# The prompt's group norm in two halves, the first under the last attention units, and output rows that begin two loop steps earlier

## The chip, the core and the metric

The kernel runs on one core of a Trainium2 chip. The metric is the device time in microseconds of one execution. A core has the engines TensorE (PE; PEld is its weight load), VectorE (DVE), ScalarE (ACT), GpSimd (POOL) and SyncE (SP), and 16 DMA engines that all of the queues share. An "x2" or "x16" of matrix rows counts instructions; one float32 matmul of the source shows as two.

## What is computed

One layer of a decoder over a prompt of 256 tokens and 8 sample tokens with a paged cache of 2048 tokens each. Heads 0 to 7 are stick-breaking ("sb"), heads 8 to 15 forgetting attention ("fox"). The part that matters here:

```python
def merge_heads(o_sb, o_fx, g_sb, g_fx, w_out):
    B, S = o_sb.shape[:2]
    o = jnp.concatenate([rms_norm(o_sb.reshape(B, S, D_SB), g_sb),
                         rms_norm(o_fx.reshape(B, S, D_FOX), g_fx)], axis=-1)
    return jnp.einsum('bse,ed->bsd', o, w_out)
...
    hp = hp + yp
    hs = hs + ys
    u = jnp.concatenate([rms_norm(hp, norm_ffn_g[l]).reshape(B * S, D),
                         rms_norm(hs, norm_ffn_g[l]).reshape(DB * DS, D)], axis=0)
    f = hier_moe(u, w_rg, b_rg, w_re, b_re, w_gate, w_up, w_down)
```

Each half of the concatenated heads has a norm of its own over its 1024 values per token. After the projection come the residual, a second norm, the routing (one of 4 groups, two of its 8 experts) and 32 experts, in float32.

## The kernel before

The middle of the kernel is one loop of 128 steps (STEPS), written out in Python for every engine, one step for each page of the sample tokens' cache: 8 sequences of 16 pages. An engine executes its own list in order and meets the others only at semaphores, so "step s" is a place in each engine's list and not a time.

In each step s:

- SP loads value page s (from s = 4, L109 to L116) and then key page s + 20 (L99 to L106), 0.5 MB for each head group, so 2 MB in a step. Both rings in SBUF hold four pages. The load of value page p waits until TensorE has used page p - 4, that of key page p until VectorE has scored page p - 4.
- TensorE multiplies value page s by the sample weights (`values`, L964).
- VectorE scores key page s + 20 against the broadcast queries (`score_page`, L128, sixteen instructions), before all else of its step. At the start of a sequence it waits for new queries (the copies by ACT at L146 of the broadcast by TensorE at L136, in step 11 of each sequence; for page 96 that is step 75).

Around these pages the prompt is worked off. Steps 0 to 71 project heads. From step UNIT0 = 16 to 79 there are 16 units of four steps (`prompt_head`): one head of causal attention, two sb heads, then two fox heads, in turn. Units 12 and 13 are the last sb heads (their outputs are copied to `qo` by step 71), 14 and 15 (steps 72 to 75 and 76 to 79) the last fox heads. A unit's last piece adds to semaphore `oc`. ACT also issues the stores of the unit's key and value rows (L1273, L1274), in pieces 1 and 2.

Then, before the change:

- step 80 (GSUM - 1): ACT squares both halves of `qo` into `xn` (L1320, waiting for all 16 units);
- steps 81 and 82: TensorE sums the squares of a half over heads and partitions, by a matrix of ones, into banks 2 and 3 (L1060);
- step 83 (GSUM + 2): VectorE takes the means (L1696), ACT the roots of both at once (L1385), VectorE the reciprocal (L1519) and 16 products in place in `qo` (L1521), one for each head;
- from step OUT = 84: `out_rows(o)` for o = 0 to 15, in two of every three steps (`out_at`), 32 matmul instructions each (L1084). o = 0 and 1 read heads 0 to 7 only, 2 and 3 heads 8 to 15, and so on in turn. Every second row step, ACT issues the next 2 MB of `w_out` (L177). VectorE adds the residual (L1527), ACT squares it (L1324), TensorE sums (L1065);
- from OUT_END = 107 the sums end, from ROUTE = 111 routing, from PLACE = 122 the placing of tokens. In steps 108 to 127 SP has only value pages left to load.

After the loop: the last sample output, the tokens of the first experts, the sample tokens' own projection, and then a second block of code with the experts, which streams 192 MB of weights. BANK R is 4 of TensorE's result banks; it holds unit rows until semaphore `row` shows that they are copied.

## Time and profile before

| | |
|---|---|
| Time, median of 3 runs | 1517.79 us (1516.69 to 1523.81) |
| Span of the profiled execution | 1514.3 us |
| TensorE, VectorE, ScalarE busy | 87%, 44%, 15% of the span |
| DMA | 377 GB/s on average, 570.4 MB in all |
| Squares (step 80) to the last output row (step 106) | 709.6 to 893.0 us |
| Last value page used | 947 us |

The span is that of one execution under the profiler; its own time is not listed beside it, and the runs are 2.4 us and more above it. The page cuts the span into 40 slices with the busy share of each engine in tenths, the granted clock of TensorE, and the share and rate of the DMA engines; the trace gives the same for any stretch. A share of the DMA engines can pass 1.00 a little, since packets overlap; 1.03 is the most that a long stretch shows.

### The profile page before, as it was taken

To read this page: it belongs to the slowest core of one execution; us is meant where nothing else is said; L and a number is where in the kernel's file an instruction comes from. 1 tells how busy PE (TensorE), PEld (TensorE's weight loads), DVE (VectorE), ACT (ScalarE), POOL (GpSimd) and SP (SyncE) were. 2 spreads that over 40 slices of the span, in tenths; PEclk is the share of its full clock that TensorE was granted. 3 is DMA by queue.
4 is the path that set the end of the run, shared out by engine and by line. 5 is a ranking of instruction groups with operands and counts; after the bars stand their busy time and mean duration, and the time that the engine had idled before them with its cause. 6 is when DMAs were issued, how large, how long until landed. Compare 5 with 4: busy or idle time off the path is not lost. (4 is left out here: it accounts for less than half of the span.)

```text
span 1514.3 us, 26133 instructions
## 1 busy us (share of the span) xinstructions
PE 1315.7 (87%) x8622; PEld 870.3 (57%) x8622; DVE 673.4 (44%) x4778; ACT 233.6 (15%) x453; POOL 75.4 (5%) x119
## 2 busy tenths in 40 slices
PE   7999788889789899856899987789999999999992
PEld 4678455566556566533667743466666565655561
DVE  4437855676676675677846466021000100000004
ACT  2111002112212212213011021101111010111011
POOL 1000000000000000001000001001100010001000
PEclk8899989899999999976999998979999999999997
DMA  9776999999999999999999989999999999999984
GB/s 302 248 260 229 385 397 391 396 383 381 382 377 390 383 379 392 387 405 398 351 403 402 401 320 390 399 414 379 422 428 428 427 424 423 422 419 414 416 341 178
DMA packets 170382, 570.39 MB, mean 377 GB/s; under 512 B 17401, under 2 KB 75562, under 8 KB 156954
## 3 DMA queue, kind: packets, MB, share of 16 engines
q1 hardware_dynamic: 145616, 541.70, 91.4%
q10 hardware_dynamic: 21762, 22.58, 4.3%
q0 software_dynamic: 2896, 4.86, 0.9%
q8 instruction: 45, 0.74, 0.2%
q14 instruction: 63, 0.52, 0.1%
HBM read 558.26 MB, written 15.67 MB: 379 GB/s over the span
## 5 line engine op out<-in xcount | busy, mean ns | idle before, releaser
L128 DVE CUSTOM_DVE_ANT_0 ws<-ws,xgT 128x128 f32<-128x128 f32 x1792 | 387.8, 284 | 204.7 <-DMA ws<-in_cache_fox_k 186.0
L979 PE MATMUL bank<-xn,ws 128*128 128x264 f32 x1152 | 289.9, 407 | 10.5 <-DMA ws<-in_w_in 10.5
L979 PEld LDWEIGHTS bank<-xn,ws 128*128 128x128 f32 x1152 | 223.0, 199 | 110.9 <-issue 54.8
L1912 PE MATMUL bank<-ws,xgT 128*64 128x256 f32 x1024 | 231.4, 386 | 16.7 <-DMA ws<-in_w_expert_up 12.1
L1914 PE MATMUL bank<-ws,xgT 128*64 128x256 f32 x1024 | 231.5, 386 | 0.0
L964 PE MATMUL bank<-ws,PR 128*32 128x512 f32 x1024 | 150.8, 668 | 78.3 <-DMA ws<-in_cache_fox_v 73.8
L1912 PEld LDWEIGHTS bank<-ws,xgT 128*64 128x64 f32 x1024 | 140.3, 139 | 104.6 <-issue 22.2
L128 DVE DVE_READ_ACCUMULATOR2_ANT Z<- 128x1 f32 x1792 | 141.8, 79 | 0.0
L1914 PEld LDWEIGHTS bank<-ws,xgT 128*64 128x64 f32 x1024 | 140.3, 139 | 0.0
L2113 DVE COPY gu<-bank 128x256 f32<-128x256 f32 x32 | 13.6, 425 | 269.4 <-PE bank L1914 269.4
L1084 PE MATMUL bank<-qo,ws 128*128 128x256 f32 x512 | 117.0, 387 | 6.2 <-DVE qo L1521 5.2
L1934 PE MATMUL bank<-ws,hT 128*32 128x512 f32 x1024 | 113.2, 594 | 7.1 <-ACT xgT L2012 6.9
L1084 PEld LDWEIGHTS bank<-qo,ws 128*128 128x128 f32 x512 | 97.7, 193 | 31.5 <-issue 16.6
L1901 PE MATMUL bank<-xg,qo 128*128 128x128 f32 x960 | 109.7, 275 | 0.0
L1901 PEld LDWEIGHTS bank<-xg,qo 128*128 128x128 f32 x960 | 108.5, 192 | 0.0
L964 PEld LDWEIGHTS bank<-ws,PR 128*32 128x32 f32 x1024 | 21.5, 112 | 119.8 <-DMA ws<-in_cache_fox_v 91.8
L523 PE MATMUL bank<-xn,ws 128*128 128x264 f32 x384 | 86.8, 387 | 0.0
L523 PEld LDWEIGHTS bank<-xn,ws 128*128 128x128 f32 x384 | 72.6, 190 | 14.1 <-issue 2.0
L1934 PEld LDWEIGHTS bank<-ws,hT 128*32 128x32 f32 x1024 | 32.0, 110 | 76.7 <-issue 67.0
L607 DVE CUSTOM_DVE_ANT_0 ws<-ws,xgT 128x128 f32<-128x128 f32 x256 | 55.3, 287 | 39.5 <-DMA ws<-in_cache_sb_k 15.6
L2120 DVE TENSOR_TENSOR hT<-si,bank 128x128 f32<-128x128 f32 x32 | 9.2, 288 | 108.3 <-ACT si L2020 108.2
L1848 POOL DMA_INDIRECT y_rows<-ys,dest x32 | 29.5, 922 | 403.6 <-DVE ys L2124 338.6
(433 smaller groups left out, 971.4 us busy)
## 6 DMA issues: line engine op xcount, KB each, us to landing
ws<-in_cache_sb_k SPq DMA_DIRECT2D x128, 512.0 KB, 9.1
ws<-in_cache_fox_k SPq DMA_DIRECT2D x128, 512.0 KB, 13.0
ws<-in_cache_sb_v SPq DMA_DIRECT2D x128, 512.0 KB, 9.2
ws<-in_cache_fox_v SPq DMA_DIRECT2D x128, 512.0 KB, 12.8
ws<-in_w_expert_gate SPq DMA_DIRECT2D x32, 2048.0 KB, 16.1
ws<-in_w_expert_up SPq DMA_DIRECT2D x32, 2048.0 KB, 20.0
ws<-in_w_expert_down SPq DMA_DIRECT2D x32, 2048.0 KB, 16.9
ws<-in_w_in SPq DMA_DIRECT2D x24, 2048.0 KB, 21.3
```

The lines of the kernel that those rows point to most:

```text
L128: ins = dve.tensor_tensor_reduce(k, k, qb[:, (g * H + h) * HD:(g * H + h + 1) * HD], 1.0, 0.0, ALU.mult, ALU.add, Z[:, n % 2, g, h, t:t + 1])
L523: mm = pe.matmul(bank[4 + k % 4][:, 0:T], chunk(n)[:, c, m * P:(m + 1) * P], xn[:, c, :], start=(c == 0), stop=(c == KC - 1))
L607: ins = dve.tensor_tensor_reduce(k, k, qb[:, (g * H + h) * HD:(g * H + h + 1) * HD], 1.0, 0.0, ALU.mult, ALU.add, Z[:, 0, g, h, t:t + 1])
L964: mm = pe.matmul(bank[0][r0:r0 + 32, :], PR[:, g, t, :], vring[:, u, g, half * 512:(half + 1) * 512], start=(t == 0), stop=(t == PAGES - 1))
L979: mm = pe.matmul(out[:, 0:T], w[:, c, m * P:(m + 1) * P], xn[:, c, :], start=(c == 0), stop=(c == KC - 1))
L1084: mm = pe.matmul(out, ws[:, 4 + r, k0:k0 + P], qo[:, 8 * r + c, 0:SEQ], start=(r == 0 and c == 0 and m % 2 == 0), stop=(r == 1 and c == 7) ...
L1848: pool.indirect_dma_start(y_half, bass.IndirectOffsetOnAxis(ap=dest[0:rows, 2 * n + k:2 * n + k + 1], axis=0), ys[k][0:rows, :], None, bou ...
L1901: mm = pe.matmul(bank[4 + k][:, c * P:(c + 1) * P], token_cols(qo, t, 4 * k + c), pick_tok[:, i, t, :], start=(t == 0), stop=(t == 1))
L1912: pe.matmul(bank[2 * k][0:SLOTS, 0:256], lhs, ws[:, wg, c * 256:(c + 1) * 256], start=(c == 0), stop=(c == KC - 1))
L1914: mm = pe.matmul(bank[2 * k][SLOTS:P, 0:256], lhs, ws[:, wu, c * 256:(c + 1) * 256], start=(c == 0), stop=(c == KC - 1))
L1934: mm = pe.matmul(bank[4 + 2 * k + dc][q * HALF:(q + 1) * HALF, :], hT[k][:, j, h0:h0 + HALF], ws[:, wd, d0:d0 + 512], start=(j == 0), stop ...
L2113: dve.tensor_copy(gu[k][:, :], bank[2 * k][:, 0:256]).then_inc(E[f"guc{k}"], 1)
```

## The change

`group_squares`, `group_sums`, the mean, the root and `group_norm` each become one call for each half. The first (sb) half runs at steps 73 (squares), 74 (sums, mean), 75 (root) and 76 (norm), under units 14 and 15, with a buffer of its own, `sb_rst`, since the other buffers share room with the units' data. The second (fox) half runs at steps 80 (squares), 81 (sums, mean, root) and 82 (norm); its sums go to bank R. The three waits of VectorE for the end of all units stand ahead of the second mean. OUT becomes 82, and with it OUT_END, ROUTE and PLACE move by two steps. In each engine's step the added calls stand behind that step's page and unit work.

```diff
--- before.py
+++ after.py
@@ -709,7 +709,8 @@
 CH, R, ZB, CB, OB = 1, 4, 5, 6, 7
 OUT_BANKS = [(2, 3), (6, 7)]
 GSUM = UNIT0 + 4 * UNITS + 1
-OUT = GSUM + 3
+SB_SUM = UNIT0 + 4 * (UNITS - 2) + 1
+OUT = GSUM + 1
 OUT_END = OUT + KC + KC // 2 - 1
 ROUTE = OUT_END + 4
 PLACE = ROUTE + 11
@@ -814,6 +815,7 @@
         take = Carve(blk)
         rst = take(2, SEQ)
         rstd = take(2, SEQ)
+        sb_rst = sb("sb_rst", [P, SEQ])
         lpart = take(SEQ)
         lg = take(2, NG + NE)
         mask, re_, tmp, oh0, oh1, rks = (take(2, NE) for i in range(6))
@@ -1056,8 +1058,10 @@
             def group_sums(g):
                 pe.wait_ge(C["gsq"], g + 1)
                 pe.wait_ge(S["evac"], 4 * TURNS)
+                if g:
+                    pe.wait_ge(S["row"], 2 * UNITS)
                 for c in range(H):
-                    mm = pe.matmul(bank[2 + g][:, 0:SEQ], ones[:, :], xn[:, g * H + c, 0:SEQ], start=(c == 0), stop=(c == H - 1))
+                    mm = pe.matmul(bank[R if g else 2][:, 0:SEQ], ones[:, :], xn[:, g * H + c, 0:SEQ], start=(c == 0), stop=(c == H - 1))
                 mm.then_inc(C["gss"], 1)
 
             def square_sums(o):
@@ -1218,8 +1222,8 @@
                     pe.matmul(bank[OB][:, 0:64], ones[:, :], QK[:, :, :], start=True, stop=True)
                     pe.wait_ge(S["lfd"], 1)
                     pe.matmul(bank[OB][:, 64:128], ones[0:NB, :], dlf[:, :, :], start=True, stop=True).then_inc(S["done1"], 1)
-                if s in (GSUM, GSUM + 1):
-                    group_sums(s - GSUM)
+                if s in (SB_SUM + 1, GSUM):
+                    group_sums(int(s == GSUM))
                 if out_at(s) is not None:
                     out_rows(out_at(s))
                 if s in (OUT_END, OUT_END + 1):
@@ -1316,8 +1320,13 @@
                 copy(osum[:, :], bank[0][:, :], "osum")
 
             def group_squares(g):
-                wait_past(act, S["oc"], UNITS)
+                wait_past(act, S["oc"], UNITS if g else UNITS - 2)
                 nc.scalar.activation(xn[:, g * H:(g + 1) * H, 0:SEQ], qo[:, g * H:(g + 1) * H, 0:SEQ], ACT.Square).then_inc(C["gsq"], 1)
+
+            def group_root(g):
+                act.wait_ge(C["gms"], g + 1)
+                root = rst[:, 1, :] if g else sb_rst[:, :]
+                nc.scalar.activation(root, root, ACT.Sqrt).then_inc(C["gsqrt"], 1)
 
             def residual_square(o):
                 act.wait_ge(C["h"], o + 1)
@@ -1377,12 +1386,14 @@
                     act.wait_ge(S["proj"], 4 * TURNS)
                     for j in range(2):
                         load_out(act, a, ws, W, j, 4 + j)
+                if s == SB_SUM:
+                    group_squares(0)
+                if s == SB_SUM + 2:
+                    group_root(0)
                 if s == GSUM - 1:
-                    for g in range(2):
-                        group_squares(g)
-                if s == GSUM + 2:
-                    act.wait_ge(C["gms"], 2)
-                    nc.scalar.activation(rst[:, :, :], rst[:, :, :], ACT.Sqrt).then_inc(C["gsqrt"], 1)
+                    group_squares(1)
+                if s == GSUM:
+                    group_root(1)
                 o = out_at(s - 1)
                 if o is not None and o % 4 >= 2:
                     for c in range(2):
@@ -1514,12 +1525,22 @@
             def red(out, x, op):
                 own.step(dve.tensor_reduce(out, x, AX, op))
 
-            def group_norm():
-                dve.wait_ge(C["gsqrt"], 1)
-                own.step(dve.reciprocal(rstd[:, :, :], rst[:, :, :]))
-                for c in range(KC):
+            def group_mean(g):
+                if g:
+                    dve.wait_ge(S["oc"], UNITS)
+                    dve.wait_ge(S["stk"], 32 * UNITS)
+                    dve.wait_ge(S["stv"], 32 * UNITS)
+                dve.wait_ge(C["gss"], g + 1)
+                dve.tensor_scalar(rst[:, 1, :] if g else sb_rst[:, :], bank[R if g else 2][:, 0:SEQ], 1.0 / (H * HD), EPS,
+                                  ALU.mult, ALU.add).then_inc(C["gms"], 1)
+
+            def group_norm(g):
+                root, rec = (rst[:, 1, :], rstd[:, 1, :]) if g else (sb_rst[:, :], sb_rst[:, :])
+                dve.wait_ge(C["gsqrt"], g + 1)
+                own.step(dve.reciprocal(rec, root))
+                for c in range(g * H, g * H + H):
                     dve.scalar_tensor_tensor(out=qo[:, c, 0:SEQ], in0=qo[:, c, 0:SEQ], scalar=gcol[:, G_GRP + c:G_GRP + c + 1],
-                                             in1=rstd[:, c // H, :], op0=ALU.mult, op1=ALU.mult).then_inc(C["on"], 1)
+                                             in1=rec, op0=ALU.mult, op1=ALU.mult).then_inc(C["on"], 1)
 
             def residual(o):
                 q, m = divmod(o, 4)
@@ -1687,14 +1708,14 @@
                 at_unit = unit_at(s)
                 if at_unit:
                     prompt_head(*at_unit)
-                if s == GSUM + 2:
-                    dve.wait_ge(S["oc"], UNITS)
-                    dve.wait_ge(S["stk"], 32 * UNITS)
-                    dve.wait_ge(S["stv"], 32 * UNITS)
-                    dve.wait_ge(C["gss"], 2)
-                    for g in range(2):
-                        dve.tensor_scalar(rst[:, g, :], bank[2 + g][:, 0:SEQ], 1.0 / (H * HD), EPS, ALU.mult, ALU.add).then_inc(C["gms"], 1)
-                    group_norm()
+                if s == SB_SUM + 1:
+                    group_mean(0)
+                if s == SB_SUM + 3:
+                    group_norm(0)
+                if s == GSUM:
+                    group_mean(1)
+                if s == GSUM + 1:
+                    group_norm(1)
                 o = out_at(s - 1)
                 if o is not None and o % 4 >= 2:
                     for c in range(2):
```

## Rows read from the trace of the kernel before

**Rows 1.** The page: TensorE and the others in all, and the DMA slices.

```profile
PE 1315.7 (87%) x8622; PEld 870.3 (57%) x8622; DVE 673.4 (44%) x4778; ACT 233.6 (15%) x453; POOL 75.4 (5%) x119
DMA  9776999999999999999999989999999999999984
```

**Rows 2.** Table by stretch: busy us and instructions of each engine, clock, DMA share, GB/s.

```profile
650.00:700.00 50.00, 27.56 (x121) 12.27 (x121) 31.15 (x231) 9.60 (x22) 0.00 (x0) 0.74 1.03 403
...
1200.00:1300.00 100.00, 95.52 (x861) 62.38 (x863) 8.43 (x19) 13.31 (x29) 11.03 (x12) 1.00 1.01 424
```

**Rows 3.** Waits of SP's queue, whole span: us in total, times, longest.

```profile
SPq L114 <- PE bank L964: 74.0, 33, 8.3
...
SPq L104 <- DVE Z L128: 35.0, 17, 9.0
```

**Rows 4.** The same table, short stretches near the change.

```profile
670.00:680.00 10.00, 1.93 (x8) 0.20 (x8) 4.20 (x35) 0.17 (x1) 0.00 (x0) 0.50 1.03 398
702.00:712.00 10.00, 6.65 (x31) 1.89 (x23) 9.86 (x83) 4.06 (x7) 0.00 (x0) 0.67 1.03 383
742.00:756.00 14.00, 14.00 (x76) 9.87 (x75) 14.00 (x133) 0.00 (x0) 0.00 (x0) 1.00 0.70 256
884.00:900.00 16.00, 16.00 (x94) 9.58 (x96) 9.88 (x71) 4.89 (x9) 0.00 (x0) 1.00 0.59 208
```

**Rows 5.** Timeline of the norm, step 83: start us, us, engine, line, [idle before].

```profile
730.00 0.75 DVE L1696 TENSOR_SCALAR blk<-bank 128x256 f32<-128x256 f32 x2
731.44 3.35 DVE L1519 RECIPROCAL blk<-blk 128x512 f32<-128x512 f32 x1 [0.69 <-ACT blk L1385]
734.83 6.42 DVE L1521 SCALAR_TENSOR_TENSOR qo<-qo,gcol,blk 128x256 f32<-128x256 f32 x16
735.46 8.73 PE L1084 MATMUL bank<-qo,ws 128*128 128x256 f32 x32 [5.22 <-DVE qo L1521]
745.40 0.33 SPq L106 DMA_DIRECT2D ws<-in_cache_sb_k  x1
```

**Rows 6.** Timeline: squares of both halves, then sums of each half.

```profile
709.64 3.71 ACT L1320 ACTIVATE xn<-qo 128x2048 f32<-128x2048 f32 x2
717.85 5.55 PE L1060 MATMUL bank<-xn,ones 128*128 128x256 f32 x16
724.33 3.72 PE L1060 MATMUL bank<-xn,ones 128*128 128x256 f32 x16
```

**Rows 7.** Timeline of ACT in steps 73 to 76.

```profile
661.75 14.35 ACTq L1273 DMA_DIRECT2D out<-blk  x1
679.83 0.49 ACT L1250 ACTIVATE blk<-bank 128x384 f32<-128x384 f32 x1 [18.22 <-issue]
690.52 0.31 ACT L1256 ACTIVATE zs<-zs 128x128 f32<-128x128 f32 x1
690.85 1.28 ACT L1283 ACT_TABLE_LOAD   x1
```

**Rows 8.** Timeline of TensorE: value page 75, broadcast, an output row step.

```profile
670.32 1.93 PE L964 MATMUL bank<-ws,PR 128*32 128x512 f32 x8 [3.73 <-DMA ws<-in_cache_fox_v]
681.88 4.69 PE L136 MATMUL bank<-xg,lastq 128*128 128x512 f32 x8
762.18 7.17 PE L1084 MATMUL bank<-qo,ws 128*128 128x256 f32 x32
893.03 1.06 PE L964 MATMUL bank<-ws,PR 128*32 128x512 f32 x8
```

**Rows 9.** Timeline of VectorE and SP: pages 96, unit 15, key load 101.

```profile
688.80 0.29 DVE L128 CUSTOM_DVE_ANT_0 ws<-ws,xgT 128x128 f32<-128x128 f32 x1 [9.20 <-ACT xgT L146]
692.20 0.29 DVE L1428 TENSOR_TENSOR sp_h<-zr,zs 128x128 f32<-128x128 f32 x1
698.56 0.42 DVE L1461 COPY blk<-bank 128x256 f32<-128x256 f32 x1 [3.28 <-DMA out<-blk]
703.59 0.33 SPq L106 DMA_DIRECT2D ws<-in_cache_sb_k  x1
```

## Prediction

> **What bounds the kernel now.** I read the slices of the page first: the DMA row is at 9 almost throughout, TensorE is 87% busy, VectorE 44% [rows 1]. The table by stretch tells them apart: the DMA share is 1.03 in 650:700, where TensorE is busy for half the time, 0.59 in 884:900, where TensorE is busy all the time, and 1.01 at 424 GB/s in the expert stage [rows 2, 4]. I take 1.03 as "full". Before the experts, then, the kernel is a stream of pages, and time is lost where the stream has a hole. SP fills it in order: at step s value page s, then key page s+20, each into a ring of four, so they wait until TensorE has consumed value page s-4 and VectorE has scored key page s+16. Whoever is late holds up both kinds. The waits of SP name both, 74.0 us on values and 35.0 us on scores [rows 3].
>
> Three places lie near the change [rows 4]:
> - Hole 1: 742:756 at a mean of 0.70 loses 14 x 0.33 = 4.6 us. Its cause is VectorE: mean, reciprocal of 512 columns (3.35 us) and sixteen products (6.42 us) keep it from scoring from 730.0 to 741.2, SP's next key load goes out at 745.40, and TensorE waits 5.22 us for the first product [rows 5].
> - Hole 2: 884:900 at 0.59 loses 16 x 0.44 = 7.0 us. VectorE is not full there. TensorE is: the last two output steps (105 and 106) stand where SP has no key pages left to load, so a step of 8.2 us (7.17 of rows, 1.06 of values; the last ends at 893.03) admits one value page of 1 MB, 2.6 us of stream [rows 4, 8].
> - 702:712, under the last two units, is full by share, but moves 383 GB/s where a full stretch moves 403: 0.5 us lost [rows 2, 4]. It matters below.
>
> Together 12.1 us. From 900 on the stream is full nearly to the last expert load [rows 2], so what is saved ahead of it shows one to one at the end.
>
> **The change, part by part.** It splits the group norm in two. The stick-breaking half: squares on ACT at step 73, sums on TensorE and the mean on VectorE at 74, root at 75, norm at 76. The other half: squares at 80, sums, mean and root at 81, norm at 82. Output rows begin at 82, not 84, and all that follows (routing, placing) moves two steps earlier. No work disappears: VectorE still has 0.75 + 3.35 + 6.42 us, TensorE 32 matmuls of sums, ACT two squares of 1.9 us; one root becomes two, and one switch of ACT's tables is added (1.28 us, below). No DMA is added; four weight loads for the output on ACT's queue go two steps earlier with their rows.
>
> (a) The first half lands in a tight place. At step 73 ACT issues the key-row stores, and these issues took 14.35 us and more: the next ACT operation began at 679.83 after 18.22 us in which it waited only for issuing [rows 7]. The new square stands behind exactly these, so it runs 679.8 to 681.7 (1.9 [rows 6]). TensorE, in step 74, now waits for it ahead of value page 75, which it took at 670.32 before [rows 8]. Its sums cost 3.72 us at full clock and 5.55 after idle time [rows 6]; the granted clock in 670:680 is 0.50, the lower level of 1.2 GHz [rows 4], and TensorE will have idled again, so I take 5.4: done at 687.2. Value page 75 to 688.2, unit 14's outputs 1.0, broadcast 3.7 at full clock (4.69 in the row) to 692.9; before, the copies of the broadcast were finished for scoring to begin at 688.80 [rows 8, 9]. With 2.1 us of copies, scoring of page 96 begins at 695.0, 6.2 us later. VectorE waits meanwhile at step 74 for the sums, and page 95 behind it has room.
>
> (b) After page 96 (3.4 us, 688.80 to 692.20) came the unit's front part, 3.1 us, a wait of 3.28 us for a store, and 0.8 us more [rows 9]. The delay eats that wait: 695.0 + 3.4 + 3.1 + 1.1 = 702.6. There the norm of the first half follows: half the reciprocal 1.75 and half the products 3.3, with starts 5.1. So page 97 is scored 707.7 to 711.1; before it was 699.4 to 702.8, and its key load went out at 703.59 [rows 9]. Now it goes at 712.0. What does the stream live on meanwhile? Before, the pause of SP until 703.59 just exhausted what was outstanding (hence the 383 GB/s). The same bytes are issued ahead of this load in both kernels, so they run out at the same time, about 705.2. **A new hole of 6.8 us** opens, with 0.2 of restart 7.0, in place of 0.5.
>
> (c) Steps 78 to 84. VectorE then has pages 98 to 101 in a row (3.4 each, with the unit's 1.5 and the denominators 0.4): 727.3. TensorE's step 81 waits for the denominators (723.9), then 2.1 of sample outputs and 4.5 of sums: 730.5. VectorE queues behind that wait (3.2 us idle), mean 0.4, page 102, totals 0.5, norm of the second half 5.1: 740.0; page 103 to 743.4, page 104 to 746.8, where it was 744.6. TensorE needs no second half for its first two output steps, so it starts rows at 731.5 instead of 735.46, does steps 82 and 83 in 8.2 us each, and has four output steps (7.17 us each [rows 8]) done by 764.4 instead of 769.3, and in step 86 instead of 88. The stream in 735:750 waits once for value page 83 on TensorE (1.1) and a little after: 1.5 us in place of 4.6, covered from 747 on by the next output weights.
>
> (d) Hole 2. The last output steps are now 103 and 104. SP, four steps ahead, still has key page 127 to send at step 107, and value pages then follow a TensorE that is free at about 881 and not 893 (150 us of its own work from 731.5). I leave 1.0 us of the 7.0. The routing chain of VectorE stands two steps earlier as well and stays under the 20 value pages that follow (52 us of stream).
>
> The tables. Around the softplus ACT loads a table at 690.85 in 1.28 us, with its neighbours back to back [rows 7]. The root of the first half puts one more such load between the softplus and unit 15's exponentials: the softplus ends at 697.2, the root at 697.2 + 1.28 + 0.4 = 698.9, and VectorE asks for it at 702.6, so it costs nothing, with 3.7 us to spare. The Trainium skill, ScalarE: Activation LUTs, section "What ACT_TABLE_LOAD costs", speaks against a root among exponentials: it counts a drain of about 1.38 us with every switch, by which an estimated 2.3 us would be to spare and the sum would stand. The row shows no such drain.
>
> **Sum.** Before 0.5 + 4.6 + 7.0 = 12.1; after 7.0 + 1.5 + 1.0 = 9.5; gain 2.6 us. The profiled execution has a span of 1514.3; the runs have 1516.7 to 1523.8 and a median of 1517.8, so 2.4 us and more lie around the span. 1514.3 becomes 1511.7, and the median 1515.2.
>
> Bounds of what the trace does not show: the new hole is 0 if stores issue without the 14 us block and the norm fits, and 6.8 + 1.8 = 8.6 if the sums run wholly at half clock (7.3 instead of 5.4). The restart of a dry stream costs 0 to 1 (a part of what 742:756 lost).
>
> **Rivals.**
> - No new hole (ACT's block ends sooner, or more is outstanding than I hold). Then after is 0.5 + 1.5 + 1.0 = 3.0, gain 9.1: 1508.7. For it: the share is 1.03 through all of 650:700, with 4 MB of output weights outstanding on ACT's queue. Against: 383 GB/s in 702:712. Chance 0.17.
> - Slower: the new hole opens, and hole 2 stays, because the stream is now late and TensorE meets its last rows with as few pages outstanding as before. Its place is VectorE's step 76 and SP's key load behind it; its price 8.6 + 1.5 + 7.0 - 12.1 = 5.0 us: 1522.8. It decides from the point at which page 97 is scored later than about 709 with hole 2 above 5 us; 0.5% needs a further 2.6 us, such as a second dry spell at 735:750 as long as now. Chance 0.15, a third of it above 0.5%.
> - The root is late: ACT's copies and softplus slip by more than those 3.7 us, and VectorE's norm waits with page 97 behind it. A slip of 6 us adds 2.3 to the hole: 1517.5. It has only the wait for unit 15's scores to hide in. Chance 0.03.
> - The shift does nothing: the expert stage is set by TensorE's chain from the last value page, or the routing chain ends last, and what the stream gains waits there. 1517.8. Against: the stream is full from 900 on. Chance 0.10.
> - Forecast as summed, 1512 to 1518: 0.55.
>
> **Numbers.** A measurement of this kernel tells about 0.5% (7.6 us) from no change. Faster by more than that needs a gain over 7.6: most of the first rival and a tail of the forecast, 0.18. Slower: 0.06. The rest, 0.76. The range takes in most of the first and the second rival: 1507 to 1522.
>
> **What would show it.** Right: a hole of 5 to 8 us near 705:713 with a key load waiting for scores; TensorE idle in step 74 with square sums behind a square at about 680; the share in 742:756 above 0.9; no stretch below 0.9 at 875:900; first output row near 731. Wrong: a full stream through 700:715 (first rival), or a share near 0.6 in 875:900 (second). It is wrong as a whole if the stream is not what the end follows: holes filled by some sum and the end moved by another.

## The result, and the profile after

The changed kernel takes **1525.55 us** (median of 8 runs, 1523.07 to 1528.7); the kernel before, in 8 runs beside it on the same chip, 1519.18. The ratio is 1.005 with a 95% interval of 1.003 to 1.007. It is slower, by 6.4 us between the medians and 7.6 by the ratio; I had forecast 2.6 us faster, with 1522 as the upper end. (One execution of a kernel below, all_warm_early, took 1946.25 us at a granted clock of 0.65 and is left out of its ratio.) The profiled execution after has a span of 1524.4, against 1514.3. A span is about 1.8 us under the time of its run, so the one before is some 3 us quicker than its kernel's median and the one after 0.6 us slower: some 3.7 of these 10.1 us are the draw of the two executions and not the change.

First the changed kernel by stretches (core us, then busy us and instructions of each engine, the granted clock, the DMA share, GB/s):

```profile
670.00:680.00 10.00, 0.00 (x0) 0.00 (x0) 0.00 (x0) 0.97 (x1) 0.00 (x0) 0.50 1.03 400
700.00:714.00 14.00, 4.72 (x32) 1.94 (x28) 13.65 (x71) 1.64 (x6) 0.00 (x0) 0.62 0.60 198
702.00:712.00 10.00, 2.86 (x17) 1.23 (x17) 9.86 (x50) 0.60 (x4) 0.00 (x0) 0.60 0.53 187
742.00:756.00 14.00, 14.00 (x76) 9.92 (x74) 11.67 (x107) 0.36 (x2) 0.00 (x0) 1.00 1.03 387
884.00:900.00 16.00, 9.90 (x52) 2.50 (x50) 10.68 (x72) 4.66 (x8) 0.00 (x0) 0.74 0.89 320
896.00:916.00 20.00, 15.00 (x100) 6.22 (x100) 11.16 (x30) 4.98 (x9) 0.00 (x0) 0.77 0.74 253
940.00:960.00 20.00, 16.97 (x77) 9.55 (x74) 6.96 (x22) 1.14 (x2) 1.49 (x2) 0.50 1.04 397
964.00:972.00 8.00, 5.26 (x40) 2.06 (x42) 0.72 (x3) 2.04 (x3) 0.00 (x0) 0.79 0.81 286
```

Beside [rows 4] this says: 702:712 fell from 383 to 187 GB/s (the new hole is there), 742:756 rose from 256 to 387 (hole 1 is gone), 884:900 rose from 208 to 320 (hole 2 is half gone; experiments 1 and 3 show that this is not all of the rows' doing). But 896:916, which the kernel before passed at this, is now a hole too, and so is 964:972:

```profile
896.00:916.00 20.00, 17.88 (x134) 7.75 (x131) 12.37 (x35) 3.86 (x7) 0.00 (x0) 1.00 0.99 382
940.00:960.00 20.00, 16.54 (x118) 11.16 (x114) 6.12 (x24) 4.27 (x7) 0.00 (x0) 0.83 1.04 390
964.00:972.00 8.00, 5.57 (x56) 1.85 (x52) 0.00 (x0) 1.20 (x2) 0.00 (x0) 1.00 1.04 387
```

**A ledger of the stream.** GB/s times the length of a stretch is what it moved. I take each kernel's MB less the kernel before's, over the same stretches up to 1100 us; 0.41 MB are taken as one us of a full stream, which moves 403 to 424 GB/s [rows 2]. Checked by the row: 700:720 moved 244 x 20 us = 4.88 MB after, 394 x 20 = 7.88 before, so -3.00 (after first, then before).

```profile
700.00:720.00 20.00, 9.23 (x48) 3.71 (x48) 19.65 (x127) 5.02 (x12) 0.00 (x0) 0.59 0.71 244
```

```profile
700.00:720.00 20.00, 14.87 (x62) 7.62 (x61) 18.83 (x165) 6.69 (x8) 6.30 (x14) 0.59 1.02 394
```

```
MB less before    640-  700-  720-  760-  880-  900-  920-  940-  960-  1000-  1060-  sum    in us   span less
                  700   720   760   880   900   920   940   960   1000  1060   1100          /0.41   before, us
after            -0.30 -3.00 +1.84  0    +1.76 -2.68 -0.26 +0.14 -1.28 -0.84   0     -4.62   11.3    +10.1
shift_only        0    -0.26 -3.56  0    +3.10 -3.02 -0.36 +0.22 -1.52 -0.84  +0.04  -6.20   15.1    +14.7
split_only       -0.24 -3.12 +1.24 -0.12 +1.60 -0.12 -0.56 -0.10 -0.92 -0.66  +0.08  -2.92    7.1     +7.1
route_kept       -0.30 -2.66 +1.12  0    +2.22 -1.06 -1.00 +0.08 -0.08 -1.14  +0.08  -2.74    6.7     +6.3
squares_first    +0.06 -1.92 +1.28  0    +1.84 -2.70 -0.98 +0.10 -0.16 -1.62  +0.08  -4.02    9.8     +9.2
norm_later       -0.30 -1.22 +1.44  0    +1.32 -2.46 -0.16 +0.06 -1.20 -0.78  -0.04  -3.34    8.1     +8.5
all_three        +0.06 -0.16 +1.00  0    +0.64 -0.84 -0.12 -0.06 -1.08 -0.78  +0.08  -1.26    3.1     +3.2
all_out84        +0.06 -0.18 +1.36 -0.12 -0.42 +0.06 -0.36 -0.02 -1.24 -0.84  +0.12  -1.58    3.9     +3.7
all_route110     +0.06 -0.14 +1.20 -0.24 +0.54 -0.78 -2.46 +0.06 -1.00 -0.78   0     -3.54    8.6     +7.7
early_sums       +0.06 +0.04 -0.12  0    +0.54 -0.08 -0.16 -0.08 +0.12 -1.44   0     -1.12    2.7     +2.1
early_sums_again +0.06 -0.14  0    -0.12 +0.62 +0.08 -0.84 +0.02  0    -1.32 +0.04 -1.60    3.9     +3.6
all_early         0    -0.02 +1.44 -0.12 +0.10 -1.08 +0.08 -0.02 -0.04 -0.42   0     -0.08    0.2     +1.7
all_warm         +0.06 -0.10 +1.08 -0.24 +0.56 -0.72 -0.56 -0.04 -1.52 -1.14  +0.08  -2.54    6.2     +5.0
all_warm_early   +0.06 +0.06 +1.12 -0.36 +0.48 -0.82 -0.54 -0.02 -0.04 +0.06  +0.04  +0.04   -0.1     -0.7
all_early_warm106+0.06  0    +0.92 -0.12 -0.36 -0.58 -0.50  0    +0.04 -0.54   0     -1.08    2.6     +2.3
all_out84_early  +0.06 -0.12 +1.28 -0.12 -0.40 +0.04 -0.30 -0.02 -0.04 +0.60   0     +0.98   -2.4     -1.8
```

The last two columns agree within 1.5 us in every row: in each profiled execution the end follows the MB moved by 1100 us. So the difference is where the stream lost its MB, and the table says where: -3.00 at the norm of the first half, -2.68 at 900:920, -1.28 and -0.84 behind 960, against +1.84 and +1.76 won at the two old holes.

Each row is one execution, and the row of the kernel before is one too. early_sums and early_sums_again are the same file: they differ by at most 0.18 MB in ten of the eleven stretches and by 0.68 in the other (920:940), and both show +0.54 or more in 880:900, ahead of anything that was edited in them. So a single entry below some 0.7 MB says little.

**The hole at 900:920.** TensorE of the changed kernel (start us, us, ..., [idle before it <- what released it]), then VectorE, then SP's value loads:

```profile
896.73 1.94 PE L966 MATMUL bank<-ws,PR 128*32 128x512 f32 x8 [1.33 <-DMA ws<-in_cache_fox_v]
901.29 0.80 PE L1041 MATMUL bank<-sp_h,tri_ge 128*128 128x128 f32 x2 [2.62 <-DVE diag L1444]
...
910.79 1.06 PE L966 MATMUL bank<-ws,PR 128*32 128x512 f32 x8 [1.65 <-ACT PR L1314]
```

```profile
898.15 1.75 DVE L1727 RECIPROCAL blk<-blk 128x256 f32<-128x256 f32 x1 [2.83 <-ACT blk L1407]
```

```profile
899.86 0.38 SPq L116 DMA_DIRECT2D ws<-in_cache_fox_v  x1
906.91 0.33 SPq L116 DMA_DIRECT2D ws<-in_cache_sb_v  x1
```

Routing is pinned to the output rows (its first step is four behind their end), so it too moved from step 111 to 109. Two steps ahead of it VectorE waits for the root of the residual (L1407) and takes the reciprocal (L1727). That used to stand at step 109; now it stands at 107, one step ahead of the step in which VectorE makes the logarithms of the last sequence (L1444). TensorE waits for these, with the value pages behind it, and SP sends no value page from 899.86 to 906.91. The wait is 2.62 us of the 6.2 in which TensorE takes no page (898.67 to 904.87). The rest is its own work: the sample's sums, as before, and now also the first products of the router ahead of this page (1.98 us), both at the lower clock (0.50 in 901:904).

### The profile page after: what moved, and what is told of

Same layout as the page of the kernel before. It is cut to its first block and busy times, and to the rows that moved or that the text cites. A ratio compares the mean times of both kernels' runs of the same rounds, so it can differ in the third digit from the quotient of the medians.

```text
span 1524.4 us, 26137 instructions
## 1 busy us (share of the span) xinstructions
PE 1326.8 (87%) x8622; PEld 877.1 (58%) x8622; DVE 673.1 (44%) x4779; ACT 235.2 (15%) x455; POOL 72.8 (5%) x119
```

## The experiments

Every kernel was timed in 5 rounds against the kernel before on its own chip; ratios are to that. Four theories stand in what was expected: H, the two new holes have causes of their own; L, the hole behind 896 comes of the stream's being late from the first; N, one cause alone makes the first hole; R, what the stream gains is lost again behind the last value page.

**1. The two parts of the change alone.** split_only keeps the norm in halves and puts the rows back; shift_only keeps the old norm and moves the rows:

```diff
 # split_only, on the changed kernel
-OUT = GSUM + 1
+OUT = GSUM + 3
 # shift_only, on the kernel before
-OUT = GSUM + 3
+OUT = GSUM + 1
```

> The changed kernel with its norm in two halves, but output rows, routing and placing where they stood before (OUT = GSUM + 3). Theory H (two holes, each with a cause of its own: the first half's sums and norm at steps 74 to 76, and routing two steps earlier that meets the last sequence's steps 107 to 109): the hole at 700:714 stays at about 8 us, the one at 742:756 is gone, 884:900 loses about 7 us as before, and 900:920 is full (share 1.0, not 0.78). Time about 3 to 5 us over before. Rival L (the hole after 896 comes from the stream being late, not from routing's place): 900:920 is hollow here as well, time as the changed kernel, 7 us over before.

> The kernel before with output rows, routing and placing two steps earlier (OUT = GSUM + 1), and the norm undivided at step 83. Theory H: nothing is lost at 700:714; the hole near 742 is 2 to 3 us larger than before, since TensorE waits for the norm with value page 83 behind it; the loss at 884:900 shrinks and one of about 5 us opens near 900:916. Time 0 to 5 us over before. Rival L: the stream is full from 890 on and the time is 2 to 5 us under before.

split_only: 1522.34 us, ratio 1.0019 (1.0002 to 1.0036). shift_only: 1529.37, ratio 1.0065 (1.0045 to 1.0086). The same stretch of each, split_only first:

```profile
896.00:916.00 20.00, 18.08 (x128) 7.38 (x127) 12.23 (x35) 5.71 (x10) 0.00 (x0) 1.00 0.93 356
```

```profile
742.00:756.00 14.00, 14.00 (x76) 9.89 (x75) 9.84 (x94) 0.00 (x0) 0.00 (x0) 1.00 0.54 187
896.00:916.00 20.00, 13.34 (x71) 4.16 (x71) 13.45 (x50) 6.42 (x10) 0.00 (x0) 0.66 0.73 260
```

L falls: split_only has the first hole in full (-3.12) and scarcely one at 900:920 (-0.12); shift_only has no first hole (-0.26) and the late one in full (-3.02). The late hole belongs to the shift. But split_only was expected to lose at 884:900 what the kernel before loses, and it did not, though its rows stand where they stood:

```profile
884.00:900.00 16.00, 16.00 (x88) 10.21 (x87) 10.66 (x79) 4.86 (x9) 0.00 (x0) 1.00 0.80 309
```

That is 309 GB/s against 208. The stream of split_only is 2.24 MB late at 880 and gains 1.60 in 880:900; that of shift_only is 3.82 late and gains 3.10. TensorE's rows set the time there (its last row step ends at 894.5 against 893.0), and a late stream still has more to send under them (SP's last key page goes at 874.62 against 871.56). So hole 2 gives part of an earlier loss back, and the +1.76 of the changed kernel (1.46 MB late at 880) is in part this, and not the work of the shift.

shift_only also shows what the split is for: with the norm whole at step 83 and rows from step 82, TensorE waits in its queue for the norm with value page 83 behind it, and 742:756 goes from 256 down to 187 GB/s. 720:760 loses 3.56 MB more than before, 8.7 us where I had expected 2 to 3, and the time is 1.0065, some 10 us over, where I had expected 0 to 5. Neither part alone is as good as the kernel before.

**2. One mend for each cause.** Each on the changed kernel alone, and all_three with the three together:

```diff
 # route_kept: routing at its old distance from the pages
-ROUTE = OUT_END + 4
+ROUTE = OUT_END + 6
 # squares_first: the square ahead of ACT's stores, its sums one step earlier
-                if s in (SB_SUM + 1, GSUM):
+                if s in (SB_SUM, GSUM):
-                if s == SB_SUM:
+                if s == SB_SUM - 1:
                     group_squares(0)
 # norm_later: VectorE's norm of the first half at step 80, not 76
-                if s == SB_SUM + 3:
+                if s == SB_SUM + 7:
                     group_norm(0)
```

> The changed kernel with its output rows two steps earlier, but routing and placing where they stood before (ROUTE = OUT_END + 6). Theory H: VectorE's root of the residual no longer stands between the last sequence's logits and its logs, TensorE does not wait for diag near 900, the share in 896:916 is above 0.95 instead of 0.74, and the time is 5 to 7 us under the changed kernel, about that of before. Rival L: 896:916 stays hollow and the time is within 2 us of the changed kernel.

> The changed kernel with the first half's squares at step 72, ahead of the stores that ACT issues at 73, and its sums at step 73 instead of 74; mean, root and norm stay. Theory H: TensorE does not wait 15 us in step 74, page 96 is scored from about 689 instead of 695, page 97 ends near 708 instead of 710.4, and 700:714 loses 4 to 5 us instead of 6 at its share of 0.60; time 3 to 4 us under the changed kernel. Rival N (only the 5 us of norm ahead of page 97 matter): the hole keeps its size and the time stays within 1.5 us.

> The changed kernel with one call of VectorE moved: the reciprocal and eight products of the first half at step 80, behind page 100, instead of step 76, ahead of page 97. Sums, mean and root stay. Theory H: page 97 is scored 5.1 us earlier, so 700:720 moves 1.8 to 2.0 MB more than the changed kernel (4.9 MB), and little is lost again at 720:760 (5 us of VectorE between pages 100 and 101 instead). Routing still meets steps 107 to 109. Time 3 to 5 us under the changed kernel. Rival N (the hole is set by the sums of step 74 alone): 700:720 stays within 0.5 MB.

> The changed kernel with squares at step 72, sums at 73, the first norm at step 80, and routing where it stood before. Theory H, by the megabytes that each stretch moves against the kernel before: 700:720 within 0.5 MB of it, 720:760 1 to 2 MB over it, 880:900 1.5 to 2 over, 900:940 1 to 2 under, so about 1 to 2 MB ahead at 960, and 3 to 5 us under the kernel before. Rival R (whatever the stream gains is lost again behind the last value page): the megabytes are gained by 880 and gone by 1060, time within 0.2% of before.

| kernel | median us | ratio | interval |
|---|---|---|---|
| route_kept | 1520.69 | 1.0018 | 1.0004 to 1.0033 |
| squares_first | 1521.95 | 1.0019 | 1.0002 to 1.0036 |
| norm_later | 1523.72 | 1.0040 | 1.0024 to 1.0056 |
| all_three | 1519.29 | 1.0006 | 0.9994 to 1.0018 |

700:714 of squares_first, then of norm_later, then of all_three:

```profile
700.00:714.00 14.00, 7.04 (x27) 2.61 (x26) 13.82 (x96) 1.64 (x5) 0.00 (x0) 0.66 0.69 260
```

```profile
700.00:714.00 14.00, 8.08 (x44) 3.12 (x40) 13.65 (x103) 4.30 (x11) 0.00 (x0) 0.70 0.90 305
```

```profile
700.00:714.00 14.00, 8.46 (x47) 3.03 (x45) 13.86 (x121) 4.88 (x7) 1.50 (x7) 0.74 1.02 383
```

From 198 GB/s to 260 by the square alone, to 305 by the norm alone, to 383 by both, where the kernel before has 389. In the ledger 1.08 and 1.78 of the 3.00 MB, and 2.84 together: the first hole had the two causes that (a) and (b) had named, and N falls. norm_later was to be 3 to 5 us under the changed kernel and is 1.5 by the ratio. route_kept takes 1.62 of the 2.68 MB at 900:920 and the wait for L1444 with it (896:916 is at 0.92, where I had expected over 0.95). It loses 0.74 MB more at 920:940, no more than two executions of one file differ there. The other 1.06 MB of the late hole are not routing's: with the rows two steps earlier and routing put back, every kernel here and below still loses 0.58 to 1.08 there (route_kept, all_three and its variants with "early" or "warm" in their names), and the three with the rows put back as well (split_only, all_out84, all_out84_early) lose 0.12 at most.

The gains in the ratio, 0.0032, 0.0031 and 0.0010, add to 0.0073, and all_three gains 0.0044. Whether the mends add up can't be told from this: each ratio is known to about 0.0015. By the spans they do (3.8, 0.9 and 1.6 us, together 6.3, against 6.9). In the ledger route_kept alone also takes 1.20 MB off the loss at 960:1000, and squares_first alone 1.12, and all three together only 0.20. That goes with the clock and not with the mend, as experiment 4 shows.

all_three is the changed kernel as it was meant: no new hole at 700, hole 1 shut, hole 2 moved more than filled. It reaches 960 us with 0.52 MB more than the kernel before (the sum of its first eight columns). And its time is the same within 0.2%, where I had expected 3 to 5 us less. R is left: -1.08 and -0.78 MB from 960 to 1060.

**3. Where the rows and the routing stand, once mended.** all_out84 is all_three with rows and routing where the kernel before has them; all_route110 moves the routing one step only.

```diff
 # all_out84, on all_three
-OUT = GSUM + 1
+OUT = GSUM + 3
-ROUTE = OUT_END + 6
+ROUTE = OUT_END + 4
 # all_route110, on all_three
-ROUTE = OUT_END + 6
+ROUTE = OUT_END + 5
```

> As all_three, but the output rows also stand where they stood before (steps 84 to 106). It tells what beginning them two steps earlier is worth once the holes under the units and at routing are out of the way. Theory H: the loss at 884:900 is 5 to 7 us again, and the time 3 to 5 us over all_three. Rival R: the same time as all_three within 0.15%.

> As all_three, with routing one step earlier than before (ROUTE = OUT_END + 5), so that the residual's root stands in step 108, behind the last sequence's logs, instead of 107, ahead of them. Theory H (the collision at 107 is one of order in VectorE's list): TensorE waits for diag less than 1 us near 900, where it waited 2.6 us, and the time is within 1.5 us of all_three. Rival (any routing earlier than step 109 collides): 896:920 is as hollow as in the changed kernel (0.74 to 0.78) and the time 4 us or more over all_three.

all_out84: 1519.2, ratio 1.0004 (0.9989 to 1.0018). all_route110: 1522.14, ratio 1.0021 (1.0004 to 1.0039). The first says that two steps of the rows are worth nothing by themselves that an interval of 0.15% to either side would show. The ledger agrees: over 880:920 all_three moves 0.16 MB more than all_out84, 0.4 us, which is within its scatter. Hole 2 is not filled in it, once the stream is not late (all_three, then before):

```profile
875.00:900.00 25.00, 19.38 (x99) 9.14 (x97) 15.77 (x110) 5.01 (x10) 0.00 (x0) 0.82 0.82 305
```

```profile
875.00:900.00 25.00, 24.78 (x129) 15.78 (x133) 15.03 (x117) 4.89 (x9) 0.00 (x0) 0.93 0.75 281
```

And all_out84, 1.12 MB ahead at 880, gives 0.42 back in 880:900 (all_out84_early, 1.10 ahead, gives back 0.40): what is won ahead of hole 2 is partly lost in it.

The second was a miss of mine: one step is slower than the kernel before (that it is slower than all_three is likely, but their intervals overlap). The wait for L1444 is gone, but another place pays:

```profile
921.30 0.64 PE L1122 MATMUL bank<-blk,tri_lt 128*128 128x32 f32 x2 [5.32 <-DVE blk L1562]
```

```profile
920.00:940.00 20.00, 15.33 (x86) 6.80 (x90) 11.83 (x42) 2.49 (x5) 2.19 (x3) 0.74 0.70 255
```

TensorE's counts wait 5.32 us for VectorE's choice of experts (the kernel before waits 1.97 us there), with value pages behind them.

**4. Behind the last value page.** TensorE there gathers the first block's tokens and projects the sample rows; SP's next loads wait for the buffers that this frees. First the kernel before, then the changed one, TensorE and SP's waits in 945:975 (us in total, times, longest):

```profile
948.68 7.39 PE L1148 MATMUL bank<-xg,qo 128*128 128x128 f32 x64
958.94 6.64 PE L1165 MATMUL bank<-ws,qo 128*32 128x512 f32 x60 [2.73 <-DVE qo L1629]
```

```profile
SPq L177 <- PE bank L1165: 10.3, 2, 9.0
```

```profile
954.76 9.84 PE L1152 MATMUL bank<-xg,qo 128*128 128x128 f32 x64
967.47 2.79 PE L1169 MATMUL bank<-ws,qo 128*32 128x512 f32 x12 [2.74 <-DVE qo L1650]
```

```profile
SPq L177 <- PE bank L1169: 14.6, 2, 13.3
```

The same 64 matmuls take 7.39 us in the one and 9.84 in the other. The granted clock in 940:960 is 0.83 before and 0.50 after (1.2 GHz, the lower level), in a stretch in which TensorE of the changed kernel waits for the DMA of nearly each value page; it is 0.50 in 954:958 and 1.00 in 962:966, so the gather began at the lower level and ended at the full one.

Which level the gather meets is no fixed trait of a kernel. Where it took 7.39 us, 960:1000 lost 0.08 MB (route_kept) and 0.16 (squares_first); where it took 9.83 to 10.29, with the end of the kernel as before, it lost 0.92 to 1.52 (after, shift_only, split_only, norm_later, all_three, all_out84, all_route110). But squares_first waits 0.49 to 0.63 us for each of its last three pages, much as the changed kernel does (0.63 to 1.00), and its clock is back in time:

```profile
953.71 7.39 PE L1152 MATMUL bank<-xg,qo 128*128 128x128 f32 x64
```

And the one file early_sums ran the first 32 matmuls of its gather in 3.82 us in one execution and in 6.25 in the other. So the 1.28 MB at 960:1000 are those of the execution that was profiled, and no edit ahead of 940 is shown to cause or to mend them.

Also, 2.73 us pass in both between gather and projection, for a root and a reciprocal. Two edits, one for each:

```diff
 # early_sums on the kernel before, all_early on all_three: in both first_tokens()
                     mm.then_inc(E["xgp"], 1)
+                    if k == 1:
+                        pe.wait_ge(C["sfox"], 1)
+                        pe.matmul(bank[2][:, 0:2 * NB], ones[:, :], sred[:, :], start=True, stop=True).then_inc(C["ssum"], 1)
...
                                          ACT.Copy).then_inc(E["xgT"], 1)
+                    if k == 1:
+                        act.wait_ge(C["sms"], 1)
+                        nc.scalar.activation(srs[:, :], srs[:, :], ACT.Sqrt).then_inc(C["ssqrt"], 1)
 # (both taken out of sample_out())
 # all_warm on all_three, all_warm_early on all_early: TensorE's step loop
+                if s >= 120:
+                    for c in range(4):
+                        pe.matmul(bank[5][:, 0:SEQ], ones[:, :], xn[:, c, 0:SEQ], start=True, stop=True)
```

> The kernel before with one change at its end: the sample rows' sum of squares on TensorE and its root on ScalarE are issued in the middle of the first block's gather (after its second bank) and not after it. In the kernel before the gather ends at 955.9 us and the sample rows' projection begins at 958.94: 3 us in which TensorE waits for that sum, its root and VectorE's scaling. Theory T (TensorE's chain behind the last value page frees the buffers of the next loads, so a microsecond on it is a microsecond of the stream): the projection begins about 956.6, the load after it at 958.7 instead of 960.92, and the time falls by 1.5 to 2.3 us, to 1516.2 to 1517. Rival D (these loads are queued deep enough that the chain is covered): the projection begins earlier all the same and the time stays within 0.5 us of the kernel before.

> The file of early_sums once more, on another occasion: its ratio was 0.9984 with an interval that touched 1. Theory T expects 0.9975 to 0.999 again; rival D 1.000.

> all_three with the same change at the end. Theory T: all_three reaches 960 us with 0.5 MB more than the kernel before and loses 1.1 MB from 960 to 1000; with the gap of about 3 us shut it loses 0.3 MB there, and the time is 1.5 to 2.3 us below all_three's 1519.3, at 1517.0 to 1517.8. Rival D: the time of all_three within 0.5 us.

> all_three with four idle products on TensorE in each step from 120 on (their results are read by nobody), so that the engine isn't idle while it waits for the last value pages. In the changed kernel the granted clock was 0.50 from 940 to 960 us and the gather of the first block took 10 us, against 0.83 and 7.2 us in the kernel before. Theory W (a stream that is ahead leaves TensorE idle, its clock drops, and the chain behind the last page takes back what the stream gained): granted clock over 0.9 from 940 to 960, gather 7.2 us, the hole at 956 to 964 (share 0.84) closed, and the time 1.5 to 3 us below all_three, 1516.3 to 1517.8. Rival D: the clock rises and the gather shortens, but the time stays within 0.5 us of all_three. Third: the idle products delay the value pages and with them the loads, and the time is 1 us or more above all_three.

> Both edits of the end together on all_three. Theories T and W: their gains add, 3 to 5 us below all_three, 1514.3 to 1516.3, which would be the fastest of the kernels here and below the kernel before (1518.5). Rival D: within 0.5 us of all_three.

| kernel | median us | ratio | interval |
|---|---|---|---|
| early_sums | 1517.16 | 0.9984 | 0.9968 to 1.0001 |
| early_sums_again | 1517.14 | 0.9995 | 0.9980 to 1.0011 |
| all_early | 1518.64 | 0.9995 | 0.9980 to 1.0009 |
| all_warm | 1520.95 | 1.0015 | 0.9999 to 1.0030 |
| all_warm_early | 1519.23 | 1.0006 | 0.9991 to 1.0021 |

The edit does on TensorE what it should (early_sums, then all_early's wait of SP, which was 14.6 us in all_three):

```profile
953.79 8.79 PE L1166 MATMUL bank<-ws,qo 128*32 128x512 f32 x80 [0.63 <-ACT xgT L1337]
```

```profile
SPq L177 <- PE bank L1170: 11.7, 2, 10.3
```

In the ledger 960:1000 goes from -1.08 MB in all_three to -0.04 in all_early. That much of theory T is shown: this chain sets these loads. It also holds with the first half of the gather at the lower clock (6.36 us in all_early, 6.25 in early_sums_again, which lost nothing there). In time it is worth 0.8 to 2.4 us by the three ratios (0.9984 and 0.9995; 1.0006 to 0.9995), each within its interval of nothing; what the forecast called 1.5 to 2.3 us is not shown.

all_warm held the clock, and the gather is back at 7.39 us, but it starts 3.6 us later than in all_three, where it took 9.83:

```profile
948.49 1.99 PE L1247 MATMUL bank<-xn,ones 128*128 128x256 f32 x8
950.32 0.95 PE L1054 MATMUL bank<-pick,osum 128*128 128x4 f32 x8
951.13 7.39 PE L1152 MATMUL bank<-xg,qo 128*128 128x128 f32 x64
```

The idle products of each step cost 1.99 us in front of the work that counts. By the trace it is the third outcome named; in time all_warm is 1.4 us over all_three by the ratios, within their intervals. So the lower clock is shown to cost 2.4 us on this chain, and holding it up this way costs more, 3.6. The two edits together, from which I had expected 3 to 5 us, stand at all_three's ratio (all_warm_early, 1.0006).

**5. The stretch 892:904 and the rows' place, once more.** all_early still moves 1.08 MB less than before in 900:920, and its clock in 892:900 is 0.50, after a wait of 4.18 us for a value page.

```diff
 # all_early_warm106, on all_early: TensorE's step loop
+                if s in (106, 107, 108):
+                    for c in range((4, 14, 4)[s - 106]):
+                        pe.matmul(bank[6][:, 0:SEQ], ones[:, :], xn[:, c, 0:SEQ], start=True, stop=True)
 # all_out84_early, on all_early
-OUT = GSUM + 1
+OUT = GSUM + 3
-ROUTE = OUT_END + 6
+ROUTE = OUT_END + 4
```

> all_early with idle products in the steps 106 to 108 (4, 14 and 4 of them), read by nobody. In all_early TensorE waits 4.2 us for the value page of 891.23, its granted clock is 0.50 from 892 to 900, and the value loads behind it come late: 1.1 MB less than before from 900 to 920. Theory W: clock 1.0 from 892 to 900, that loss shrinks to 0.5 MB or less, and the time falls by 1 to 1.5 us, to 1517.1 to 1517.6. Rival: the stretch is bound by VectorE's and ScalarE's chain for the last sequence's weights, which no clock of TensorE shortens: the clock rises, the loss stays at 1 MB, and the time is all_early's within 0.5 us.

> all_early with the projection at the place of the kernel before (step GSUM + 3), so that of the changed kernel only the norm of one group under the units is left, with the three mends and the earlier sample sums. If the shift of the projection by one step is worth nothing by itself (the pages behind the last key page take 2.6 us of stream each, an output step 8.2 us, so that a hole opens in either place), the time is that of all_early within 1 us, 1518 to 1519.5; if the shift costs through the two output steps that then collide with other work, 1 to 2 us less, 1516.5 to 1517.5; if it gains, 1 to 2 us more.

all_early_warm106: 1518.61, ratio 1.001 (0.9992 to 1.0028). The clock is 1.0 and the loss at 900:920 falls from 1.08 to 0.58 MB, but the fourteen products took 6.31 us, more than the 4.2 they were to fill:

```profile
887.75 6.31 PE L1248 MATMUL bank<-xn,ones 128*128 128x256 f32 x28
893.99 1.07 PE L966 MATMUL bank<-ws,PR 128*32 128x512 f32 x8
```

The page behind them was taken at 893.99, where all_early took it at 891.23, and 880:900 and 920:940 lost 0.46 and 0.58 MB more. The experiment was badly sized (fourteen products in 4.2 us would be 0.3 us each, and they take 0.45) and settles nothing on the clock there.

all_out84_early: 1514.36 (median of 12), ratio 0.9989 (0.9974 to 1.0005), the lowest median of all, and 0.9 us under all_early by the ratios: the first of the outcomes named, that the shift is worth nothing by itself. Of the change only the split norm is left in it, mended, with the earlier sample sums. It moves 0.98 MB more than the kernel before by 1100 us and has none of the new holes (the execution profiled is close to its median):

```profile
700.00:714.00 14.00, 9.93 (x44) 4.17 (x48) 13.86 (x122) 4.88 (x7) 0.00 (x0) 0.62 1.02 378
742.00:756.00 14.00, 14.00 (x73) 10.84 (x73) 10.85 (x101) 0.00 (x0) 0.00 (x0) 1.00 1.01 396
880.00:896.00 16.00, 16.00 (x88) 10.49 (x87) 11.43 (x87) 4.86 (x9) 0.00 (x0) 1.00 0.56 197
896.00:916.00 20.00, 17.36 (x136) 7.36 (x128) 13.43 (x39) 4.47 (x8) 0.00 (x0) 1.00 1.02 392
```

It is surely faster than the changed kernel (intervals 0.9974 to 1.0005 and 1.003 to 1.007 don't touch); that it beats the kernel before is likely and not shown. Hole 2 (880:896) is deeper than ever in it, 197 GB/s against 231 before.

## Why the prediction was wrong, step by step

- **What bounds the kernel**: right as far as the stream goes. The ledger gives the span within 1.5 us in all fifteen other kernels.
- **(a), the square behind ACT's stores**: right nearly to the number. Square expected 679.8, was 679.03; sums to 687.2, were done 687.6; page 96 at 695.0, was 695.10.

```profile
679.03 1.91 ACT L1324 ACTIVATE xn<-qo 128x2048 f32<-128x2048 f32 x1 [18.19 <-issue]
680.99 6.60 PE L1064 MATMUL bank<-xn,ones 128*128 128x256 f32 x16 [15.17 <-ACT xn L1324]
695.10 0.29 DVE L128 CUSTOM_DVE_ANT_0 ws<-ws,xgT 128x128 f32<-128x128 f32 x1 [2.88 <-issue]
```

- **(b), page 97 and the new hole**: right. Page 97 began at 707.24 (707.7 forecast) and its key load went at 711.46 (712.0). The hole cost 3.00 MB in 700:720, 7.3 us, where the sum had 6.5 net; squares_first and norm_later showed both causes.

```profile
702.30 1.73 DVE L1540 RECIPROCAL sb_rst<-sb_rst 128x256 f32<-128x256 f32 x1
704.07 3.25 DVE L1542 SCALAR_TENSOR_TENSOR qo<-qo,gcol,sb_rst 128x256 f32<-128x256 f32 x8
707.24 0.28 DVE L128 CUSTOM_DVE_ANT_0 ws<-ws,xgT 128x128 f32<-128x128 f32 x1
...
711.46 0.33 SPq L106 DMA_DIRECT2D ws<-in_cache_sb_k  x1
```

- **The tables**: right. The root's load and its neighbours stand back to back (1.28 us at 695.53, 697.15 and 698.88), and the root was done at 698.86, 3.4 us ahead of VectorE's reciprocal. No drain shows between them. The Trainium skill, ScalarE: Activation LUTs, section "What ACT_TABLE_LOAD costs", counts about 1.38 us of drain with every switch to another set; this trace differs, and the measurement decides.
- **(c), steps 78 to 84**: right. First row at 730.92 (731.5), hole 1 shut, +1.84 MB or 4.5 us at 720:760, where the sum had 3.1.
- **(d), hole 2 and the routing: the step that failed.** I took 6.0 us from hole 2 and put the routing at nothing. Of the 6.0 us 4.3 seemed to come (+1.76 MB at 880:900), but by luck in part: split_only has +1.60 there with the rows unmoved, because its stream is late, and between all_three and all_out84 the shift is worth 0.4 us over 880:920. And I wrote that the routing chain "stays under the 20 value pages that follow (52 us of stream)". What covers a late VectorE is not the pages still to come but what SP has outstanding, at most the ring of four, and TensorE takes these pages in one queue with the waits for VectorE. The residual's reciprocal in front of the logarithms of the last sequence, and the router's products ahead of the page, held that queue, SP was silent for 7 us, and 2.68 MB, 6.5 us, were lost in 900:920: 1.62 MB of them go when routing is put back, and about 1 MB only when the rows are put back too. What in the rows' place costs this 1 MB stays open. I had looked at where each chain ends and not at what stands behind it in the same step, though (d) says itself that it moves. shift_only shows the loss without the split, route_kept shows the larger part going with the routing, and split_only all of it with rows and routing.
- **"From 900 on the stream is full, so what is saved ahead of it shows one to one"**: wrong as well. [rows 2] prints no stretch between 700 and 1200; in the kernel before the share is 0.99 to 1.04 in 900:1000 and 0.96 in 1000:1060, with TensorE's chain behind the last page just under it. In the changed kernel's profiled execution that chain ran 2.4 us longer at the lower clock and the stream lost 1.28 MB (3.1 us) in 960:1000; in all_three, 0.5 MB ahead at 960, it lost 1.08. And hole 2 takes back part of what is saved ahead of it (all_out84: 0.42 of 1.12 MB). My rival "the shift does nothing" named this mechanism, at 0.10.

The sum by the ledger, in us of stream at 0.41: 0.7 ahead of 700, 7.3 at the first hole, 6.5 at 900:920, 0.6 at 920:940, 3.1 and 2.0 behind 960, less 4.5, 4.3 and 0.3 gained; 11.1 us, against a span longer by 10.1, of a change of 6.4 to 7.6 us in the times. My slower rival (1522.8) had the right sign with another mechanism: the late stream did not keep hole 2 open but helped to fill it, and another one opened behind it.

What stays open: the 0.4 to 1.6 MB by which 1000:1060 differs among kernels with no edit there (early_sums lost 1.44 and 1.32 MB in it, all_out84_early gained 0.60), whether the half clock costs the 1.08 MB of all_early at 900:920, and which of the kernels whose intervals hold 1 is the fastest.

## What to carry to other kernels

A delay on a stream through a ring is covered at most by what the ring holds, four pages here, and not by all that is still to come; ask of each moved step which waits stand behind it on each engine's queue. When one constant is tied to another (the routing to the end of the rows), a shift moves everything tied to it, so list these and look for what each now stands in front of. Before counting a gain, follow it to the end of the kernel: MB moved per stretch, kernel against kernel, shows in one table where a gain is made and where it is handed back. Profile one file twice before reading small entries of such a table, and run the half of the change that should leave a hole alone: a hole that another engine sets can fill because the stream is late, and that is no gain.

## What the runs showed of the hardware

- DMA issues on an engine's own queue hold back its computing. In the changed kernel ScalarE's square stood 18.19 us behind store issues (14.33 and 3.66 us, behind two weight loads issued at 659.87 and 660.32), while TensorE waited 15.17 us for it. Put ahead of the same stores (squares_first) it ran at 660.80, TensorE waited 1.81 us for it, and the stores behind it blocked ScalarE for the next 16.63 us instead.
- TensorE that had waited for its stream ran at the lower clock into the work that came next: 64 matmuls took 9.84 us (clock 0.50 in 940:960) against 7.39. It is not so in each execution (7.39 in squares_first, after waits of 0.49 to 0.63 us). In all_early the same gather went through both levels in one piece, 32 matmuls in 6.36 us and the next 32 in 3.82:

```profile
949.24 6.36 PE L1152 MATMUL bank<-xg,qo 128*128 128x128 f32 x32
955.44 0.29 PE L1157 MATMUL bank<-sred,ones 128*128 128x16 f32 x2
955.58 3.82 PE L1152 MATMUL bank<-xg,qo 128*128 128x128 f32 x32
```

- A product of 128x128 by 128x256 in 32-bit floats is two instructions of the trace, 0.45 to 0.5 us together at full clock (28 in 6.31 us), so that idle products are dear: that spoiled one experiment and decided another.
